# Gate vector's first four tiles in other places, its sum in SBUF, five of its eight sums inside the channel transform, its columns in the second output tile

## The reference

```python
sh1, sc1, gt1, sh2, sc2, gt2 = ada_params(c, w_mod[i], b_mod[i])   # silu(c) @ w_mod + b_mod, split in six
a_lat = modulate(h_lat, g_norm_mix[i], sh1, sc1)                   # rms_norm * (1 + scale) + shift
f = jnp.fft.fft2(ag, axes=(1, 3), norm="ortho").real               # over 512 tokens and 256 channels of a group
y_lat = f.astype(a.dtype).reshape(B, L, D) @ w_out
h_lat = h_lat + gt1 * y_lat
h_lat = h_lat + gt2 * conv_ffn(modulate(h_lat, g_norm_ffn[i], sh2, sc2), ...)
```

## Time and profile before

| | us |
|---|---|
| three runs: median (lowest to highest) | 1448.54 (1448.4 to 1450.48) |
| profiled execution: its time | 1448.21 |
| profiled execution: span of the core | 1446.3 |
| PE busy | 1414.6 |
| POOL busy | 784.3 |
| DVE busy | 519.9 |
| ACT busy | 502.9 |

### The profile page before, as it was taken

One profiled execution on the slowest core, in us unless ns is written; L12 is line 12 of the kernel. 1 busy time (PEld: TensorE's weight loads), 2 busy tenths in 40 slices (PEclk: granted clock), 3 DMA queues, 4 the chain that ended last, 5 costly groups with the idle time before them and its releaser, 6 DMA issues.

```text
span 1446.3 us, 21820 instructions
## 1 busy us (share of the span) xinstructions
PE 1414.6 (98%) x8140; PEld 1157.2 (80%) x8140; DVE 519.9 (36%) x713; ACT 502.9 (35%) x712; POOL 784.3 (54%) x1038
## 2 busy tenths in 40 slices
PE   7989999999999999999999999999999999999997
PEld 5768888888888788888888867878788888888887
DVE  5876332222003832222200368975444222221003
ACT  5334333333123433233212367335433332332122
POOL 1753645554555855555554577563566554554553
PEclk9999999999999999999999999999999999999999
DMA  9963333223222332322323222200133233223221
GB/s 365 404 243 117 116 116 116 87 102 99 90 102 73 102 102 93 104 94 92 101 98 102 73 90 74 73 17 3 60 102 117 87 99 102 89 94 105 92 73 59
DMA packets 45129, 156.44 MB, mean 108 GB/s; under 512 B 5264, under 2 KB 8080, under 8 KB 44944
## 3 DMA queue, kind: packets, MB, share of 16 engines
q1 hardware_dynamic: 45072, 155.63, 31.5%
HBM read 153.51 MB, written 2.10 MB: 108 GB/s over the span
## 4 chain that ended last, share of the span: by engine, by line
PE 84%; DVE 8%; issue 3%; ACT 3%; POOL 1%; DMA 0%; SPq 0%; DVEq 0%; POOLq 0%; ACTq 0%
PE ps L1873 26%; PE ps L1875 26%; PE ps L1874 26%; POOL w_lo L606 1%; DVE tri_p L1299 1%; DVE tri_x L1299 1%; PE ps L2357 1%; ACT w_hi L808 1%; DVE mid_sq L1302 1%; DVE act_lo L1302 1%; PE ps L2413 0%; PE ps L1889 0%; DVE rAR L1302 0%; DMA x_tok<-tokens 0%; DVE pads L1299 0%
## 5 line engine op out<-in xcount | busy, mean ns | idle before, releaser
L606 POOL TENSOR_TENSOR w_lo<-raw,w_hi 128x256 fp32r<-128x256 f32 x932 | 688.8, 772 | 550.1 <-ACT w_hi L808 549.9
L1873 PE MATMUL ps<-act_hi,w_hi 128*128 128x512 f32 x1328 | 522.0, 393 | 3.7 <-DVE act_lo L1302 2.0
L1875 PE MATMUL ps<-act_hi,w_lo 128*128 128x512 f32 x1328 | 517.0, 389 | 0.0
L1874 PE MATMUL ps<-act_lo,w_hi 128*128 128x512 f32 x1328 | 516.8, 389 | 0.0
L808 ACT ACTIVATE w_hi<-raw 128x1024 fp32r<-128x1024 f32 x233 | 245.0, 1054 | 424.5 <-PE ps L1875 401.8
L1873 PEld LDWEIGHTS ps<-act_hi,w_hi 128*128 128x128 f32 x1328 | 249.3, 188 | 63.5 <-issue 5.7
L1875 PEld LDWEIGHTS ps<-act_hi,w_lo 128*128 128x128 f32 x1328 | 249.3, 188 | 52.4
L1874 PEld LDWEIGHTS ps<-act_lo,w_hi 128*128 128x128 f32 x1328 | 249.3, 188 | 52.1 <-issue 1.4
L1873 PE MATMUL ps<-hid_hi,w_hi 128*128 (+2 forms) x584 | 219.2, 375 | 0.0
L1875 PE MATMUL ps<-hid_hi,w_lo 128*128 (+2 forms) x584 | 218.7, 374 | 0.0
L1874 PE MATMUL ps<-hid_lo,w_hi 128*128 (+2 forms) x584 | 218.7, 374 | 0.0
(11 more groups left out here) (298 smaller groups left out, 962.4 us busy)
## 6 DMA issues: line engine op xcount, KB each, us to landing
raw<-weight_units SPq DMA_DIRECT2D x233, 512.0 KB, 3.5
wm_mid<-mod_units SPq DMA_DIRECT2D x18, 512.0 KB, 8.6
wm_ring<-mod_units SPq DMA_DIRECT2D x9, 512.0 KB, 15.1
wm_late<-mod_units SPq DMA_DIRECT2D x8, 512.0 KB, 8.4
wm_early<-mod_units SPq DMA_DIRECT2D x5, 512.0 KB, 9.1
x_tok<-tokens SPq DMA_DIRECT2D x4, 512.0 KB, 5.6
wm_first<-mod_units SPq DMA_DIRECT2D x4, 512.0 KB, 11.5
wm_w<-mod_units SPq DMA_DIRECT2D x4, 512.0 KB, 16.7
```

What stands on the lines that cost most here:

```text
L606: ins = nc.gpsimd.tensor_tensor(w_lo[:, slot, c], raw[:, slot, c], w_hi[:, slot, c].bitcast(f32), SUB)
L1873: nc.tensor.matmul(o, wh, xh, start=start, stop=False, **check)
L1874: nc.tensor.matmul(o, wh, xl, start=False, stop=False, **check)
L1875: return nc.tensor.matmul(o, wl, xh, start=False, stop=stop, **check)
```

## The change

It does five things. GT1's first four tiles (16 to 19) get slots that no longer lie on data of the sequence transform (`wm_early` places 4 to 6, which SC1's tiles leave, and a new place 27, `wm_side`), so SP issues them before its wait for the transform, which moves to tile 20. GT1's sum runs in SBUF (`mod_acc`) and not in PSUM; SC1's and SH1's small transposes use `mod_acc2`. Five of GT1's eight sums move forward on DVE. GT1's addition over partitions on PE moves from the fourth output tile to the second, SH2's to the start of the seventh. The sums of SH2 and SC2 behind the `xT` tiles are spread anew, and the last of DVE's two additions of squares goes behind the last `xT` tile.

```diff
-SUMS_BEHIND = (0, 0, 2, 0, 3, 5, 3, 0)
+SUMS_BEHIND = (1, 1, 2, 2, 3, 3, 1, 0)
...
-MID_SLOTS = (7, 8, 9, 10, 11, 12, 13, 14, 2, 0, 1)
+GT1_SLOTS = (4, 5, 6, 27, 7, 8, 9, 10)
+GT1_FLAGS = (4, 5, 6, 10, 7, 8, 9, 10)
+MID_SLOTS = (11, 12, 13, 14, 2, 0, 1, 7, 8, 9, 10)
...
-            n = flag = MID_SLOTS[(i - 2 * KT) % len(MID_SLOTS)]
+            n = flag = MID_SLOTS[(i - 3 * KT) % len(MID_SLOTS)]
...
+        wm_side = view("wm_side", [P, 1, D], o_act + 4 * (2 * KT * T - D))
...
-        mod_accs = {SH1: (mod_acc, None), SC1: (mod_acc2, None), ...}
+        mod_accs = {SH1: (mod_acc2, None), SC1: (mod_acc2, None), ...}
...
-            return ps[...] if vv in (GT1, SH2, SC2) else acc_of(vv)
+            return ps[...] if vv in (SH2, SC2) else acc_of(vv)
...
             for i in range(2 * KT, 5 * KT):
-                if i == 2 * KT:
+                if i == 2 * KT + 4:
                     sp.wait_ge(sem("seq_mm"), KT)
                 load_wm(i)
                 if i == 3 * KT - 1:
                     sp.wait_ge(sem("wm_rows"), rows_through(2 * KT - 1))
+                    sp.wait_ge(sem("wm_used"), sums_through(2 * KT + 2))
                     sp.dma_start(xT[:, :, :], a_xt).then_inc(sem("loaded_once"), 16)
...
             after(sem("loaded_vec"), 16)
+            wm(2 * KT)
             mod_out(SC1)
...
             f_sums(0)
+            wm(2 * KT + 1)
             f_sums(1)
+            wm(2 * KT + 2)
             f_sums(2)
+            wm(2 * KT + 3)
             f_sums(3)
...
             tt(dc_tiles(act_lo), dc_products(), dc_tiles(act_hi).bitcast(f32), SUB, "y_lo")
+            wm(2 * KT + 4)
             for t in range(6, KT):
                 f_sums(t)
             for t in range(F_POOL, KT):
                 f_low(t)
-            for i in range(2 * KT, 3 * KT):
+            for i in range(2 * KT + 5, 3 * KT):
                 wm(i)
             after(sem("chan_mm"), KT + 1)
-            for i in range(3 * KT, 3 * KT + 3):
-                wm(i)
+            wm(3 * KT)
             mod_out(GT1)
+            wm(3 * KT + 1)
+            wm(3 * KT + 2)
...
                     x0_sum(KT - 3)
-                    x0_sum(KT - 2)
+            x0_sum(KT - 2)
...
-            MOD_TILES = {3: (GT1, 0), 6: (SH2, KT // 2)}
+            MOD_TILES = {1: (GT1, 0), 6: (SH2, 0)}
```

More of the change, by code:

```diff
@@ L166, in wm_places @@
             n, flag = EARLY_SLOTS[i], EARLY_FLAGS[i]
+        elif i < 3 * KT:
+            n, flag = GT1_SLOTS[i - 2 * KT], GT1_FLAGS[i - 2 * KT]
         elif i < 5 * KT:
-            n = flag = MID_SLOTS[(i - 2 * KT) % len(MID_SLOTS)]
+            n = flag = MID_SLOTS[(i - 3 * KT) % len(MID_SLOTS)]
         else:
@@ L464, in wm_buf @@
         def wm_buf(n):
-            tensor, first = [x for x in ((wm_ring, 0), (wm_early, 3), (wm_mid, 7), (wm_mid2, 13), (wm_late, 15), (wm_first, 19), (wm_w[0], 23), (wm_w[1], 25)) if x[1] <= n][-1]
+            tensor, first = [x for x in ((wm_ring, 0), (wm_early, 3), (wm_mid, 7), (wm_mid2, 13), (wm_late, 15), (wm_first, 19), (wm_w[0], 23), (wm_w[1], 25), (wm_side, 27)) if x[1] <= n][-1]
             return tensor[:, n - first, :]
         warm = view("warm", [P, 3 * P], o_hid + 4 * (FT * T + TT_ * (D + NY) + KT * NY + 2 * KT + 16))
-        mod_accs = {SH1: (mod_acc, None), SC1: (mod_acc2, None), GT1: (mod_acc, None), SH2: (mod_acc3, None), SC2: (mod_acc, GT1), GT2: (mod_acc3, SH2)}
+        mod_accs = {SH1: (mod_acc2, None), SC1: (mod_acc2, None), GT1: (mod_acc, None), SH2: (mod_acc3, None), SC2: (mod_acc, GT1), GT2: (mod_acc3, SH2)}
         def acc_of(vv):
@@ L475, in running_sum @@
         def running_sum(vv):
-            return ps[:, ACC_BANK:ACC_BANK + 2, :].rearrange("p b t -> p (b t)") if vv in (GT1, SH2, SC2) else acc_of(vv)
+            return ps[:, ACC_BANK:ACC_BANK + 2, :].rearrange("p b t -> p (b t)") if vv in (SH2, SC2) else acc_of(vv)
         hi_done, lo_done = sem("hi_done"), sem("lo_done")
```

## The result

| | before | changed |
|---|---|---|
| median of the runs (lowest to highest), us | 1448.47 (1447.97 to 1450.48, 4 runs) | 1467.46 (1465.7 to 1468.39, 4 runs) |
| profiled execution, us | 1448.21 | 1466.96 |
| span of the core, us | 1446.3 | 1465.1 |

The changed kernel is slower: ratio 1.0128, 95% interval 1.0115 to 1.014. Direction and place were as forecast, the size was not: 14.0 us were forecast, 19.0 were lost, and the time lies above the range. At the first matmul of the first FFN the two kernels are 18.4 us apart (126.92 against 108.50); the spans differ by 18.8.

What follows compares the result with a forecast made beforehand. PE bounds the kernel, busy for 98% of the span. Late dc, 13.7 us, plus 0.3 (second-tile stall against the end's gain) make 14.0 on 1448.2: 1462.2 us, range 1458.7 to 1465.0.

Steps and rivals of the forecast that it cites:

- Part 1: At SC1's mod_out: tile 16 still lands at 40.0, DVE waits 16 us, SH1's rows on PE start 11.1 us late.
- rival A: Not slower: tile 16 lands early, so no first wait; DVE 1.6 us late at dc; 1450.1 us, chance 0.04.
- B: Faster: tile 16 early, new sums cost dc and second tile nothing, PE's end waits go; 1445.6 us, chance 0.02.
- Part 2: Behind PE's 11 us pause: slow pace, 0 to half of 6.4 us; PE's path to dc 11.1 to 14.3 late.
- Part 3: In the channel transform: three sums over tiles 17 to 19 lengthen DVE's chain; dc 13.7 us late (13.2 to 14.8).
- Part 4: At the second output tile: GT1's columns wait for DVE's sum over tile 23; stall 2.9 us (2.0 to 3.8).
- Rival D: DVE and POOL hold each other up on SBUF sums: dc 14.8 late, later terms +1.3; 1464.3 us, chance 0.14.
- Part 5: End of the projection: PE's waits of 1.19 and 1.62 go, gain of 2.6 us; net +0.3 with the stall.
- Rival C: Only the first wait, 11.1 us, costs; new sums hide, second-tile stall is least, -0.6; 1458.7 us, chance 0.10.

Runs made afterwards that it cites:

- e1: Changed kernel with the sum over tile 16 moved from ahead of SC1's mod_out to behind the first f_sums; 1458.81 us, ratio 1.0064.
- e3: Changed kernel with tile 16 given place 27 and its own semaphore and loaded early, right behind tile 7; 1458.16 us, ratio 1.0063.
- e4: Changed kernel with 20 filler matmuls on PE ahead of SH1's rows, DVE's transpose waiting for them; 1466.12 us, ratio 1.012.
- h1: Changed kernel with filler matmuls in all three PE pauses: ahead of SH1's rows, the dc wait and the second output tile; 1464.21 us, ratio 1.0109.
- f1: Changed kernel with POOL's act_lo of tiles 1 to 5 held until DVE has made dc_lo; 1465.03 us, ratio 1.0108.
- f3: Changed kernel with GT1's columns back in the fourth output tile and its mod_out back behind three sums; 1467.3 us, ratio 1.0121.
- g2: Changed kernel with the edits of g1 and f3 together; 1460.63 us, ratio 1.0087.
- g1: Changed kernel with GT1's running sum going to PSUM from tile 20 on; 1463.7 us, ratio 1.0106.
- e2: Kernel before with only tile 16 in the new place, loaded ahead of SP's wait, its sum ahead of SC1's mod_out; 1462.47 us, ratio 1.0095.

## Why the prediction was wrong in size

**Part 1 was right.** Tile 16 landed at 40.3 (40.0 forecast), DVE waited 16.15 us, the rows came 11.35 late. e1 and e3 show that this wait, and not the sum, is the cause. Rivals A and B, which needed an early tile, are out. e3 gives the tile early, as rival A has it, and measures not 1450.1 but 1458.2: DVE then waits 2.81 us for tile 17, which A did not price, and A had the same hole at dc and behind it as the forecast.

**Part 2 is the step that failed.** It named the pace after a pause, priced it at up to 3.2 us, and let it run beside DVE's chain, "does not add". For the first pause that holds: e4 and h1 leave dc where it was, since DVE's list does not wait for PE there. But Parts 3 and 4 each create a further wait of PE, and behind those no DVE chain runs along. The pace was never asked there. It cost 1.4 behind the 1.83 wait (h1 and f1, by two different edits) and 1.6 from the stall on (h1; 0.2 of it in the moved rows, 0.86 instead of 0.64): 2.9 of the 4.2 us. The prediction had the pace from the kernel's start, where the granted clock reads 1.00 all the same; here the windows show the drop.

**Part 3 was mis-sized**, dc at 15.35 and not 13.7. The three sums were inside the forecast, 1.49, 1.29 and 1.28 us, 4.06 together for 4.0 to 4.5. What was not in the sum are two operations of 8 elements per partition that the change does not touch: shifted to another time, they met an `act_lo` of POOL and ended with it, 1.8 us longer together than before. f1 takes this away and dc moves 2.05. Rival D had the mechanism, but priced it only for the large operations.

**Part 4 was right for half a reason.** The stall and the moved rows were 0.4 longer than forecast. The stall was put down to DVE alone; f3 shows that POOL, whose `w_lo` the SBUF sums slowed, would have held PE 2.75 us anyway. Only both edits together (g2) remove it. The Trainium skill, page "SBUF — State Buffer", section "Who interferes with whom", says that a DVE instruction with two SBUF inputs contends with a GpSimd one that reads SBUF, and that what they share is an exclusive lock. The trace agrees: the two small operations end with POOL's `act_lo`, f1 has them at 0.17 us without it, and g1 has `w_lo` at 0.78 instead of 1.46.

**Part 5 was right**: 3.05 came back for a forecast 2.6, and no wait is left behind the eighth tile. Rival C (1458.7) fell with DVE's chain, as argued.

With these terms put in, 13.7 + 1.65 + 1.5 + 2.9 + 0.4 + 1.1 - 3.05 = 18.2, the measured lateness at the sums of squares. About 0.6 of the 18.8 of the span comes behind that mark; it was not looked into. Nor was it tried whether the two small operations meet POOL in every execution: g1's and g2's profiles show them free, h1's shows one of them held up, and why is open. Why the clock stayed low for longer behind the shorter stalls of f3 and g1 is open too.

## What to carry to other kernels

When a change makes a late engine wait, add to each new wait the slow pace behind it, and ask for each separately whether something hides it: here 1.4 us behind a wait of 1.8. A sum moved into an engine's idle time is only free if its data has landed, it does not hold up a busy neighbour (`w_lo` at 1.46 us instead of 0.78), and the instruction that ends the next wait does not stand behind it. When removing one cause of a stall gives nothing, look who arrives next and remove both. And before a gain is put down to an edit, compare the stretches that the edit can reach: of g1's 3.8 us none lay there.

## What the runs showed of the hardware

In these runs the loss of pace did not follow the length of the pause. From dc to the projection PE lost 1.4 us after 1.83 us without work, and 2.5 after 4.95 (e3, 5.29 against 2.77); from SH1's rows to dc it lost 1.5 after 10.65 (e2). Behind the second tile's stall, h1, where the clock stayed at 1.00, needs 41.7 us from that tile's first matmul to the sums of squares. The changed kernel, after 4.08 us, needs 43.05 (77.09 to 120.14); f3, after 2.75 us, needs 45.33, of which 0.6 are GT1's columns. In all of these stretches but h1's the windows have a granted clock of 0.50 to 0.92, a mix of the two levels of 1.2 and 2.4 GHz.

The addition of SH1's bias and `dc_lo`, 8 elements in each partition, took 0.17 and 0.17 us in f1, 0.40 and 0.27 in the kernel before, 1.29 and 1.17 in the changed kernel; the two long ones ended with an instruction of POOL. A load issued 10 us earlier behind the same loads was there no earlier, at 40.3 against 40.05.
